# Pairs of feed-forward chunks: four adjacent ones per layer, their sums and transfers in another order

## The reference

```python
def swiglu(x, w_gate, w_up, w_down):
    return (jax.nn.silu(x @ w_gate) * (x @ w_up)) @ w_down

u = rms_norm(h, ffn_norm_g[i])
h = h + swiglu(u, ffn_w_gate[i], ffn_w_up[i], ffn_w_down[i])     # 1024 -> 2816 -> 1024
gate = jax.nn.sigmoid(rms_norm(h, ple_norm_g[i]) @ ple_w_gate[i])
h = h + gate * (p[i] @ ple_w_proj[i])
```

## Time and profile before

| | us |
|---|---|
| median of 3 runs | 1067.34 |
| lowest and highest run | 1065.82, 1068.52 |
| profiled execution | 1071.25 |
| its span | 1069.4 |
| PE busy in it | 1010.9 |
| DVE busy | 722.3 |
| ACT busy | 565.5 |
| POOL busy | 156.4 |

### The profile page before, as it was taken

One profiled execution on the slowest core, in us unless ns is written; L12 is line 12 of the kernel. 1 busy time (PEld: TensorE's weight loads), 2 busy tenths in 40 slices (PEclk: granted clock), 3 DMA queues, 4 the chain that ended last, 5 costly groups with the idle time before them and its releaser, 6 DMA issues.

```text
span 1069.4 us, 13573 instructions
## 1 busy us (share of the span) xinstructions
PE 1010.9 (95%) x5422; PEld 854.5 (80%) x5422; DVE 722.3 (68%) x858; ACT 565.5 (53%) x685; POOL 156.4 (15%) x124
## 2 busy tenths in 40 slices
PE   9999929999989999992999998999999999999997
PEld 8977828888878888881888887888888888999886
DVE  6986638687857776763878775666554476777664
ACT  6326516566546777651655655665444543434533
POOL 4892510000010311161000001100000000000000
PEclk9999969999999999996999999999999999999999
DMA  8766877876644533457778654466555445455531
GB/s 317 227 203 114 289 198 232 279 252 228 228 151 163 187 130 119 172 202 206 245 259 274 233 199 158 158 226 236 180 195 197 157 163 191 176 187 191 197 118 40
DMA packets 33406, 210.55 MB, mean 197 GB/s; under 512 B 4024, under 2 KB 6584, under 8 KB 9280
## 3 DMA queue, kind: packets, MB, share of 16 engines
q1 hardware_dynamic: 24768, 173.55, 44.4%
q0 software_dynamic: 5552, 32.96, 12.1%
q10 hardware_dynamic: 3024, 3.18, 1.1%
HBM read 206.46 MB, written 3.21 MB: 196 GB/s over the span
## 4 chain that ended last, share of the span: by engine, by line
PE 84%; POOL 4%; DMA 4%; DVE 4%; ACT 2%; issue 2%; ACTq 0%; POOLq 0%; DVEq 0%
PE bank L395 56%; PE bank L517 11%; PE bank L381 4%; PE bank L383 4%; PE bank L382 4%; DMA arena<-in_ws 3%; PE bank L431 2%; DVE bank L2000 2%; POOL w_lo L1010 1%; POOL q_lo L1090 1%; PE bank L532 1%; DMA u_scr<-arena 1%; POOL arena L1087 1%; POOL arena L1086 1%; PE bank L622 1%
## 5 line engine op out<-in xcount | busy, mean ns | idle before, releaser
L1720 DVE TENSOR_TENSOR w_lo<-raw,w_hi 128x2048 fp32r<-128x2048 f32 x151 | 353.0, 2344 | 139.0 <-ACT w_hi L1177 138.5
L1177 ACT ACTIVATE w_hi<-raw 128x2048 fp32r<-128x2048 f32 x162 | 309.6, 1912 | 142.2 <-PE bank L395 112.7
L395 PE MATMUL bank<-w_hi,x_hi 128*128 128x512 f32 x608 | 167.1, 397 | 0.2
L395 PE MATMUL bank<-w_lo,x_hi 128*128 128x512 f32 x608 | 162.9, 390 | 0.0
L395 PE MATMUL bank<-w_hi,x_lo 128*128 128x512 f32 x608 | 162.9, 390 | 0.0
L395 PEld LDWEIGHTS bank<-w_hi,x_lo 128*128 128x128 f32 x608 | 114.1, 188 | 24.4
L395 PEld LDWEIGHTS bank<-w_lo,x_hi 128*128 128x128 f32 x608 | 114.1, 188 | 24.0
L395 PEld LDWEIGHTS bank<-w_hi,x_hi 128*128 128x128 f32 x608 | 110.6, 188 | 23.4 <-issue 1.8
L395 PE MATMUL bank<-w_hi,z_hi 128*128 128x512 f32 x320 | 94.3, 394 | 6.0 <-DVE z_lo L1814 5.9
L395 PE MATMUL bank<-w_hi,z_lo 128*128 128x512 f32 x320 | 92.8, 390 | 0.0
L395 PE MATMUL bank<-w_lo,z_hi 128*128 128x512 f32 x320 | 92.8, 390 | 0.0
(11 more groups left out here) (280 smaller groups left out, 1373.2 us busy)
## 6 DMA issues: line engine op xcount, KB each, us to landing
raw<-in_ws SPq DMA_DIRECT2D x162, 1024.0 KB, 4.9
arena<-in_ws POOLq DMA_DIRECT2D x24, 1024.0 KB, 10.0
arena<-u_scr ACTq DMA_DIRECT2D x16, 142.0 KB, 6.1
arena<-in_rows POOLq DMA_DIRECT2D x2, 1024.0 KB, 5.3
toep<-bias_row POOLq DMA_DIRECT2D x1, 1536.0 KB, 34.9
h<-in_x_tok SPq DMA_DIRECT2D x2, 512.0 KB, 4.0
raw<-in_ws SPq DMA_DIRECT2D x2, 512.0 KB, 7.8
arena<-in_rows POOLq DMA_DIRECT2D x2, 512.0 KB, 4.9
```

What stands on the lines that cost most here:

```text
L395: ins = pe.matmul(dst, tok(a_part, k, t), w_part[:, s, c], start=first and j == 0 and i == 0, stop=last and j == 2 and i == len(ks) - 1)
L1177: act.activation(w_hi[:, g % SPLIT, :], operand(g), ACT.Copy).then_inc(hi_done, 1)
L1720: dve.tensor_tensor(w_lo[:, g % SPLIT, :], operand(g), w_hi[:, g % SPLIT, :].bitcast(F32), ALU.subtract).then_inc(lo_done, 1)
```

## The change

- `STEPS` becomes 0, 1, (2, 3), (4, 5), (6, 7), (8, 9), 10: four pairs next to each other. Each of the later three does the down-projections of the pair before.
- `q_f32` moves from slot 0 to slot 1 (offset 7168). For a layer's first pair, the load of T1's first half goes out before the sums of the tokens, and its accumulation after them, ahead of `q_lo`; then T4.
- T3 is T2 plus B21 by an accumulating transfer on POOL (`third_sum`), read from the weights in memory; the DVE's third sum and SP's wait for T3 are gone.
- The second sum for the next pair is made on DVE inside the pair before, between two of its splits. For the first pair it waits for `q_lo`.
- PE waits for `q_lo` after the first product and the first transposes. Pairs swap banks 0 and 1 from one to the next (`b1 = n % 2`); the first single uses banks 0 and 1, the second 0 and 2, the last 1 and 2.
- In the last step, the transposes of chunks 8 and 10 come one down-projection earlier, on PE, ACT and DVE alike.

```diff
-STEPS = (0, 1, (2, 3), 4, (5, 6), 7, (8, 9), 10)
+STEPS = (0, 1, (2, 3), (4, 5), (6, 7), (8, 9), 10)
...
-WITHIN = {(2, 3): (0, 1), (5, 6): (2, 4), (8, 9): (5, 7)}
-BEHIND = {4: (3,), 7: (6,), 10: (9, 8, 10)}
-TURNED = {(2, 3): (1, None), (5, 6): (2, 4), (8, 9): (5, 7), 1: (0,), 4: (3,), 7: (6,), 10: (9,)}
+WITHIN = {(2, 3): (0, 1), (4, 5): (3, 2), (6, 7): (5, 4), (8, 9): (7, 6)}
+BEHIND = {10: (9, 8, 10)}
+TURNED = {(2, 3): (1, None), (4, 5): (3, 2), (6, 7): (5, 4), (8, 9): (7, 6), 1: (0,), 10: (9,)}
...
-        q_f32 = view(5120, 4, 4, P)
+        q_f32 = view(7168, 4, 4, P)
...
-                                ready=ready_from(m) if i == 0 else None, at=1 if i > 1 else 0,
+                                ready=ready_from(m) if i == 0 else None, at={0: (0, 1), 1: (0, 2), GU - 1: (1, 2)}[i],
...
-                    for j, k in enumerate(BEHIND.get(i, ())):
-                        if j:
-                            hidden_job(k)
+                    behind = BEHIND.get(i, ())
+                    for j, k in enumerate(behind):
+                        if j + 1 < len(behind):
+                            hidden_job(behind[j + 1])
                         down(k)
...
-                    if n == NPAIR * layer + 1:
-                        pe.wait_ge(S("q_lo"), layer + 1)
-                    b1, b2, b4 = 0, 2, 1
+                    b1, b2 = n % 2, 2
+                    b4 = 1 - b1
                     turned, within = TURNED[p], WITHIN[p]
                     product(("p1", n), ffn_at(layer, p, "B11"), *of_x(0, t0), b1, True, (S("c_11"), 2 * n - 1))
                     hidden_job(turned[0])
+                    if n == NPAIR * layer + 1:
+                        pe.wait_ge(S("q_lo"), layer + 1)
                     product(("p5", n), ffn_at(layer, p, "T1"), *of_q(0), b4, True, (S("c_22"), 2 * n - 1))
...
+            def second_part(name, layer, p):
+                n = pair_no(layer, p)
+                if name == "T1":
+                    pool.wait_ge(S("t1_in"), 32 * n - 16)
+                    pool.dma_start(sums[:, 0, :], ws[B12_ROW[layer, p]], accum_op=ALU.add).then_inc(S("t1_in"), 16)
+                else:
+                    pool.wait_ge(S("t4_in"), 32 * n - 16)
+                    pool.dma_start(sums[:, 2, :], ws[PIECE_OF[ffn_at(layer, p, "B22")]], accum_op=ALU.add) \
+                        .then_inc(S("t4_in"), 16)
-            def input_sums(m):
+            def first_sums(m):
+                layer, p = PAIRED.index(m), PAIRS[0]
+                pool.dma_start(sums[:, 0, :], ws[PIECE_OF[ffn_at(layer, p, "B11")]]).then_inc(S("t1_in"), 16)
...
                 pool.tensor_tensor(q_f32[:, 3, :, :], a11, a21, ALU.subtract).then_inc(S("q_sums"), 1)
+                second_part("T1", layer, p)
                 pool.wait_ge(S("q_hi"), layer + 1)
                 pool.wait_ge(S("q_sums"), layer + 1)
                 pool.tensor_tensor(flat4(q_lo), flat4(q_f32), flat4(q_hi).bitcast(F32), ALU.subtract).then_inc(S("q_lo"), 1)
+                for n_ in range(2):
+                    for t in range(TT):
+                        pool.wait_ge(*jobs[(m, n_, t)])
+                pool.dma_start(sums[:, 2, :], ws[B12_ROW[layer, p]]).then_inc(S("t4_in"), 16)
+                second_part("T4", layer, p)
+            def third_sum(layer, p):
+                lo_ready(pool, ffn_at(layer, p, "T2"))
+                pool.dma_start(sums[:, 1, :], ws[PIECE_OF[ffn_at(layer, p, "B21")]], accum_op=ALU.add) \
+                    .then_inc(S("t3_in"), 16)
...
+                for before, p in zip(PAIRS, PAIRS[1:]):
+                    lo_ready(pool, ffn_at(layer, before, "T1"))
+                    sum_there(pool, layer, before, "T2")
                     pool.dma_start(sums[:, 0, :], ws[PIECE_OF[ffn_at(layer, p, "B11")]]).then_inc(S("t1_in"), 16)
+                    third_sum(layer, before)
+                    second_part("T1", layer, p)
+                    lo_ready(pool, ffn_at(layer, before, "T4"))
+                    pool.dma_start(sums[:, 2, :], ws[B12_ROW[layer, p]]).then_inc(S("t4_in"), 16)
+                    second_part("T4", layer, p)
+                third_sum(layer, PAIRS[-1])
...
                     ahead(o)
+                    while left:
+                        left.pop()()
...
                     gated(two, 0, c_12[:, 256:512])
-                    third_sum(p)
                     ahead(o + 4)
...
                     ahead(o + 7)
+                    if p != PAIRS[-1]:
+                        second_sum(PAIRS[PAIRS.index(p) + 1])
                     ahead(o + 8)
```

More of the change, by code:

```diff
@@ L300, in sum_there @@
             else:
-                eng.wait_ge(S("t3"), n)
+                eng.wait_ge(S("t3_in"), 16 * n)
         def col(name, i=0, n=1):
@@ L334, in _ @@
                                 sum_there(sp, layer, p, "T2")
-                            if old == ffn_at(layer, p, "B21"):
-                                sum_there(sp, layer, p, "T3")
                 if g == HELD_PIECE:
@@ L401, in wait_job, with token_chunk @@
                     pe.wait_ge(*jobs[key])
-            def token_chunk(key, g0, a_hi, a_lo, ready=None, between=None, release=None, hooks={}, at=0):
+            def token_chunk(key, g0, a_hi, a_lo, ready=None, between=None, release=None, hooks={}, at=(0, 1)):
                 for a in range(2):
@@ L407, in token_chunk @@
                     for t in range(TT):
-                        b = at + t
+                        b = at[t]
                         if ready:
@@ L769, in _ @@
             token_chunk(("pw2", 1), G["pw2"] + 2, z_hi, z_lo, between=lambda: h_jobs(0, 0), release=h_release(0, 1),
-                        at=6)
+                        at=(6, 7))
             ffn(0, 0)
@@ L1074, in h_factor, with flat4 @@
                 pool.tensor_tensor(st2[:, 2 * m:2 * m + 2], st2[:, 58:60], st2[:, 56:58], ALU.pow).then_inc(S("r_done"), 1)
-            def input_sums(m):
-                layer = PAIRED.index(m)
+            def flat4(z):
+                return z.rearrange("p i k c -> p (i k c)")
+            def second_part(name, layer, p):
[10 more added lines that the diff above has]
+                pool.dma_start(sums[:, 0, :], ws[PIECE_OF[ffn_at(layer, p, "B11")]]).then_inc(S("t1_in"), 16)
                 for n_ in range(2):
@@ L1090, in input_sums @@
                 pool.tensor_tensor(flat4(q_lo), flat4(q_f32), flat4(q_hi).bitcast(F32), ALU.subtract).then_inc(S("q_lo"), 1)
-            def flat4(z):
-                return z.rearrange("p i k c -> p (i k c)")
-            def weight_sums(layer):
[L1097 to L1104, removed]
-                    pool.dma_start(sums[:, 0, :], ws[PIECE_OF[ffn_at(layer, p, "B11")]]).then_inc(S("t1_in"), 16)
[L1106 to L1116, removed]
@@ L1118, in _ @@
             h_factor(0)
-            input_sums(0)
+            first_sums(0)
             weight_sums(0)
@@ L1137, in _ @@
             h_factor(3)
-            input_sums(3)
+            first_sums(3)
             weight_sums(1)
@@ L1265, in single @@
                                        ACT.Copy).then_inc(S("q_hi"), 1)
-                    for j, k in enumerate(BEHIND.get(i, ())):
-                        if j:
-                            hidden_hi(k)
+                    behind = BEHIND.get(i, ())
+                    for j, k in enumerate(behind):
+                        if j + 1 < len(behind):
+                            hidden_hi(behind[j + 1])
                         ahead(ffn_at(layer, "down", k))
@@ L1830, in second_sum @@
                         lo_ready(dve, ffn_at(layer, PAIRS[PAIRS.index(p) - 1], "T3"))
+                    else:
+                        dve.wait_ge(S("q_lo"), layer + 1)
                     sum_there(dve, layer, p, "T1")
@@ L1834, in second_sum @@
                     dve.tensor_tensor(sums[:, 1, :], sums[:, 0, :], raw[:, g % RAW, :], ALU.add).then_inc(S("t2"), 1)
[L1836 to L1842, removed]
                 def single(i):
@@ L1857, in single @@
                             ahead(g + 1)
[L1858 to L1863, removed]
+                    if i == 1:
+                        second_sum(PAIRS[0])
+                    behind = BEHIND.get(i, ())
+                    for j, k in enumerate(behind):
+                        if j + 1 < len(behind):
+                            hidden_lo(behind[j + 1])
                         ahead(ffn_at(layer, "down", k))
```

## The result

The changed kernel takes 1043.62 us (median of 4 runs, 1042.61 to 1044.09), the kernel before beside it 1067.01: a ratio of 0.978, interval 0.976 to 0.980, or 23.4 us less. The forecast was 28.1 us less. The profiled execution took 1044.09, its span 1042.3, so 27.1 less than the span before; 4.4 us of that lie ahead of the feed-forward block, in code that the change leaves alone: POOL starts on layer 0's norm factor at 112.76 and not at 117.14. They come from the single executions that were profiled and not from the change: in the second trace of the changed kernel (`after_again`) the same step starts at 115.14, and the profiled execution of before was 3.9 us over its median. From that point on the traces differ by 22.7 us, 7.8 in layer 0 and 14.9 in layer 1.

A forecast was written before the change was run, and what follows sets the result against it. PE, busy 95% of the span, was taken as the bound. Terms: -(18.8 + 12.2) - 5.4 - 5.9 + 10.2 + 4 = -28.1 us, taking the median from 1067.34 to 1039 us; forecast range 1031 to 1046, overall 1031 to 1058.

The forecast's parts named there:

- Step 1, the gap: At each layer's first pair, T1's early load shortens PE's gap: 12.2 us gained in layer 0, 18.8 in layer 1.
- the price of the accumulation "of its own": At a layer's start, T1's accumulating transfer, running alone, lands in about 7.4 us.
- The clock fell in layer 0 as forecast: After layer 0's gap the next product runs at the lower clock, taken as 5.37 us; 13.8 us gained if it stays.
- Step 2, one product: Chunks 4 and 7, singles before, join pairs: one product fewer per layer, 5.4 us gained in two layers.
- Step 3, the ends: At the layer's end, earlier transposes of chunks 8 and 10 remove all four PE waits: 5.9 us gained.
- Step 4, the third sum off DVE: In each pair DVE loses 2.28 us of work: zero gain, but cover for the handovers between pairs.
- Step 5, the bank: At three handovers between pairs per layer, PE waits 1.7 us for a bank: 10.2 us lost.
- Step 6, the transfers: Between adjacent pairs, transfers exceed the interval by 2.3 us, three times per layer; leads cover part: 4 us lost.
- The balance of 34.9 against 32.6 us per interval: Between pair starts, two loads and three accumulations plus q0's or q1's pieces need 34.9 us of all engines within 32.6.
- The slower rival: POOL's queue serializes each pair's transfers; slower from 38.5 us an interval on, 1092 us at 42; chance 0.06.
- The bandwidth rule of the Trainium skill: For transfers between pairs, a limit of about 358 GB/s per core: none late, the sum 4 us better.
- The rival in which DVE holds POOL's transfers up: POOL writes transfers only between DVE's two-input operations, costing about 2.5 us at six handovers: 1055 us; chance 0.04.

The follow-up runs named there:

- experiment 2: Changed kernel with POOL's two bias table loads in layer 0 issued after the feed-forward block's sums: 1039.89 us, ratio 0.973 to the kernel before.
- experiment 3: Changed kernel with the transposes of chunks 8 and 10 back right before their own down-projection: 1052.99 us, ratio 0.986 to the kernel before.
- experiment 5: T3 summed on DVE again: in the changed kernel alone 1044.62 us; with the last quarter also made ahead of T2's split, 1032.43 us.
- experiment 7: Changed kernel with last quarter first, bias table loads late, each layer's first T1 added on DVE: 1029.88 us; with T3 on DVE too, 1019.06 us.
- Experiment 1: Changed kernel with the pair before's last quarter (silu, gated product) made ahead of T2's split on ACT and DVE: 1039.6 us, ratio 0.974.

## Why the prediction was right, and where its steps were off

The direction, the range and the mechanism held; the sum was 4.7 us too large by the medians. That it was no further off is luck in part: the gap gave 7.4 us less than forecast, and the 4 us that the transfers were to cost did not come. By its own steps:

- **Step 1, the gap**: 31.0 us forecast, 23.6 measured from PE's end of chunk 1 to the end of the third product: 30.6 to 22.3 in layer 0 (132.56 to 154.9), 30.4 to 15.1 in layer 1 (470.2 to 485.3). The term that was off is the price of the accumulation "of its own", 7.4 us; it was 10.34 and 10.51, and in experiment 2 10.66 and 9.55. The forecast took the queueing behind T4's load as gone. But now a piece of SP's goes through first: in layer 0 q1 moves 1.06 MB from 132 to 136 us and has 72.5% of the engines (layer 1 alike, 1.00 MB from 462 to 466), and only then does POOL's queue have them to itself. By the forecast's own terms that is 7.4 + 2.9 = 10.3 us. The queues from 132 to 136, and the window behind it:

```profile
q1 hardware_dynamic: 149, 1.06, 72.5%
q0 software_dynamic: 13, 0.11, 29.2%
```

```profile
138.00:140.00 2.00, 0.00 (x0) 0.00 (x0) 0.00 (x0) 0.00 (x0) 0.00 (x0) 1.00 1.00 209
```

  In layer 0, T1's load was also 0.7 us ahead of PE's end of chunk 1 and not 2.5, as its 17.9 us were 16.1 in the plan. The clock fell in layer 0 as forecast, though the product took 4.3 us and not 5.4; it also fell in layer 1, where I had it kept: after 4.3 us of waiting the product took 4.5 us.
- **Step 2, one product**: 5398 matmuls, and pairs as long as before; 5.4 us.
- **Step 3, the ends**: all four waits went, and experiment 3 brought them back.
- **Step 4, the third sum off DVE**: worth nothing, as said, and not needed as cover either: experiments 5 and 7 put it back, and PE waits for DVE no longer than before (two new waits, for ACT, of 0.3 us in experiment 5). In the changed kernel it was an exchange of idle DVE time for transfers that were short.
- **Step 5, the bank**: 1.7 us at six places forecast, 1.74 to 1.75 measured (10.5). Experiment 1 showed the order to be the cause.
- **Step 6, the transfers**: 4 us forecast, 0 measured (experiment 5). The balance of 34.9 against 32.6 us per interval was near but too high: from 215.6 to 248.4 the ten transfers (10.49 MB) took 1.02 x 32.8 = 33.5 us of the engines. The share was 0.99, 1.03 and 1.02 in layer 0's three intervals, so they were short by less than 1 us each, and the leads carried that. What was off is where it shows: at 31 us an interval, once the bank waits are gone, it costs about half of what they had (experiment 1). The slower rival, POOL's queue with an interval of 38.5 us or more, had 0.06 and did not show; one load more per pair, with its wait, brings it (39.0 and 41.8).

The parts measured give -23.6 - 5.4 - 5.9 + 10.5 + 0.7 (two waits of 0.33 for B22's lo part in a layer's first pair) = -23.7 us, against -22.7 in the traces from the norm factor on; 1 us is not placed. The bandwidth rule of the Trainium skill (DMA: Bandwidth & Descriptors, Specifications) foretold no late transfer, and in the changed kernel's trace neither ACT nor DVE waited for one between pairs (ACT did at the start of each layer, 19.8 us in two). But at 320 to 332 GB/s, under the rule's limit, the engines' share was already 1.02 to 1.03, so in this mix of loads and accumulations that limit is not what fills them. The rival in which DVE holds POOL's transfers up did not show: with DVE busy 83 of 100 us, issues of accumulations took 841 to 927 ns.

## What to carry to other kernels

When a schedule is packed tighter, price the parts alone: here the headline of the change cost 6 us or more net as it was written, and the moves made along with it brought all the gain. An in-order queue makes small work (0.47 us) wait behind large splits; put what frees a resource first. And a resource at its limit that costs nothing yet should be relieved before the wait that hides it is removed: the quarter's order alone gave 4 to 6 us, the sum moved back to an idle engine alone gave nothing, both together gave 11 to 12 us.

## What the runs showed of the hardware that was not expected

- An accumulating transfer fills all 16 engines at about 200 GB/s (share 1.00 at 209 GB/s in the window above), where 141 to 143 us of before, mostly plain loads, show 418 at share 0.99. At the start of a layer, where a plain piece goes beside it, 1 MB of it landed after 9.6 to 10.7 us.
- The clock fell after a wait of 1.87 us in experiment 1 (four matmuls in 1.83 and 1.91 us, 1.07 at full clock), with no other wait of PE for 80 us ahead of it. It also fell after single waits of 1.82 us (experiment 5, T3 alone: granted clock 0.57 from 184 to 188 us), 2.25 (experiment 1, layer 1), 2.90, 3.09 and 3.17 us. It did not after the waits of 1.74 to 1.75 us that came every 33 us in the changed kernel. Whether the length of the wait alone decides was not tried.
- A DVE split that started while POOL made q_lo ended only behind it: the split of B11 took 5.02 us (at 128.24 in the last fence of experiment 7), where 2.28 to 2.29 is usual. In that trace q_lo ended at 131.10 and the split 2.2 us later; in the kernel before a split of 5.01 us ended 2.2 us after q_lo too.
